# The scan's closing step of a quarter, with one multiply-and-add of 64 columns per head and term

## The reference

```python
y_diag = einsum('bcgij,bcgrij,bcjgr,bcjgrp->bcigrp', cb, decay, dt, x)
states = einsum('bcjgn,bcjgr,bcjgrp->bcgrpn', Bm, decay_to_end * dt, x)
h      = chunk_decay * h + states                  # carried from chunk to chunk
y_off  = einsum('bcign,bcigr,bcgrpn->bcigrp', Cm, exp(acs), h_prev)
y = y_f + flip(y_b) + d_skip[:, None] * xs         # forward, backward, skip
y = rms_norm(y * silu(z), ssd_norm)
```

## Time and profile before

| | |
|---|---|
| median of 3 runs | 1747.11 us (1747.05 to 1749.56) |
| the profiled execution | 1745.69 us, its span 1744.0 us |
| PE busy | 1610.1 us (92%) |
| VectorE busy | 1025.2 us (59%) |
| ScalarE busy | 675.2 us (39%) |
| GpSimd busy | 99.4 us (6%) |
| mean granted clock of PE | 0.96 of 2.4 GHz |
| chain that ended last | PE 76%, VectorE 12%, ScalarE 7% |

### The profile page before, as it was taken

One profiled execution on the slowest core, in us unless ns is written; L12 is line 12 of the kernel. 1 busy time (PEld: TensorE's weight loads), 2 busy tenths in 40 slices (PEclk: granted clock), 3 DMA queues, 4 the chain that ended last, 5 costly groups with the idle time before them and its releaser, 6 DMA issues.

```text
span 1744.0 us, 27356 instructions
## 1 busy us (share of the span) xinstructions
PE 1610.1 (92%) x11141; PEld 1525.7 (87%) x11141; DVE 1025.2 (59%) x1416; ACT 675.2 (39%) x1149; POOL 99.4 (6%) x155
## 2 busy tenths in 40 slices
PE   3699999998999899898979999999999999999998
PEld 2599999988999798888866579999989999999998
DVE  5476666664856467888856644334964253353468
ACT  4544444332446226666736543332432121121120
POOL 1000011110010110000000000000000000000000
PEclk9699999999999899999989999999999999999999
DMA  9244444443276766767661034534222222223231
GB/s 326 91 141 142 142 135 163 150 137 123 91 229 207 243 205 217 252 185 223 192 235 63 1 109 167 181 118 153 81 73 73 77 69 76 71 73 99 72 98 61
DMA packets 159747, 241.55 MB, mean 139 GB/s; under 512 B 8049, under 2 KB 126561, under 8 KB 156577
## 3 DMA queue, kind: packets, MB, share of 16 engines
q1 hardware_dynamic: 136464, 171.45, 30.3%
q0 software_dynamic: 12304, 47.72, 7.3%
q10 hardware_dynamic: 10880, 20.97, 4.5%
HBM read 195.06 MB, written 45.06 MB: 138 GB/s over the span
## 4 chain that ended last, share of the span: by engine, by line
PE 76%; DVE 12%; ACT 7%; issue 3%; DMA 1%; SPq 0%; ACTq 0%; DVEq 0%
PE acc L833 61%; PE tp L833 12%; DVE arena L2027 2%; ACT arena L1656 2%; ACT whi L1430 1%; PE tp L1215 1%; DVE wlo L1927 1%; DVE arena L2180 1%; DMA arena<-in_w_mod 1%; PE tp L916 1%; DVE wlo L1978 1%; DVE arena L2182 1%; DMA y_nat<-arena 1%; ACT arena L1442 1%; ACT whi L1793 1%
## 5 line engine op out<-in xcount | busy, mean ns | idle before, releaser
L833 PE MATMUL acc<-hh,whi 128*128 128x322 f32 x1152 | 305.2, 326 | 20.5 <-DVE wlo L1927 7.2
L833 PE MATMUL acc<-hl,whi 128*128 128x322 f32 x1152 | 299.1, 321 | 0.0
L833 PE MATMUL acc<-hh,wlo 128*128 128x322 f32 x1152 | 297.5, 320 | 0.0
L833 PEld LDWEIGHTS acc<-hh,whi 128*128 128x128 f32 x1152 | 210.0, 199 | 23.0 <-issue 10.4
L1927 DVE TENSOR_TENSOR wlo<-raw,whi 128x2048 fp32r<-128x2048 f32 x74 | 169.4, 2290 | 93.6 <-ACT whi L1430 93.6
L833 PEld LDWEIGHTS acc<-hl,whi 128*128 128x128 f32 x1152 | 210.4, 198 | 0.0
L833 PEld LDWEIGHTS acc<-hh,wlo 128*128 128x128 f32 x1152 | 209.9, 198 | 0.0
L1430 ACT ACTIVATE whi<-raw 128x2048 fp32r<-128x2048 f32 x74 | 141.0, 1907 | 167.0 <-PE acc L833 167.0
L833 PE MATMUL acc<-whi,hh 128*128 128x256 f32 x640 | 185.4, 290 | 0.0
L833 PE MATMUL acc<-wlo,hh 128*128 128x256 f32 x640 | 182.0, 284 | 0.0
L833 PE MATMUL acc<-whi,hl 128*128 128x256 f32 x640 | 182.0, 284 | 0.0
(11 more groups left out here) (292 smaller groups left out, 2948.9 us busy)
## 6 DMA issues: line engine op xcount, KB each, us to landing
raw<-in_w_in SPq DMA_DIRECT2D x38, 1024.0 KB, 7.0
raw<-in_w_mlp SPq DMA_DIRECT2D x32, 1024.0 KB, 5.2
arena<-in_w_mod SPq DMA_DIRECT2D x24, 1024.0 KB, 6.4
arena<-decay_sums_t ACTq DMA_DIRECT2D x40, 512.0 KB, 5.5
arena<-xs_nat SPq DMA_DIRECT2D x8, 1024.0 KB, 7.8
raw<-in_w_ssd_o SPq DMA_DIRECT2D x8, 1024.0 KB, 6.0
y_nat<-arena POOLq DMA_DIRECT2D x6, 1024.0 KB, 7.1
arena<-y_nat SPq DMA_DIRECT2D x6, 1024.0 KB, 6.0
```

The source lines that it names most:

```text
L833: return pe.matmul(out, l, r, start=first, stop=last)
```

## The change

`carried` is written with scalar_tensor_tensor, (a x s) + b, where s is one number per partition; so each instruction takes one head's 64 columns. The forward term stays one multiply over 512 columns. Then eight instructions (chunks 1 to 3 only) make hF = hF x decay + states, eight make y = backward x factor + y, and after a wait for them eight make y = x times skip + y. carried_ok is signalled by the last instruction of the backward term, and VectorE itself waits for it ahead of the skip term. The scratch tq and the helper `skipped` are still used by the context chunk.

```diff
@@ -2192,18 +2192,18 @@
                                     (("y_out0", 16), ("sq_ok", 8)))[c - 1]:
                         dve.wait_ge(s[name], n)
                 y = y_of(c)
-                dve.tensor_tensor(y[:, h], v(tp[:, 2]), f4(dec[:, c, 0], q), ALU.mult)
-                if c < NT - 1:
-                    do(dve.tensor_tensor(tq, v(tp[:, 3]), f4(dec[:, c, 0, NH:], q), ALU.mult))
-                    dve.tensor_tensor(hF[:, h], hF[:, h], f4(dec[:, c, 2], q), ALU.mult)
-                    do(dve.tensor_tensor(y[:, h], y[:, h], tq, ALU.add))
-                    dve.tensor_tensor(hF[:, h], hF[:, h], v(banks(q)[1]), ALU.add).then_inc(car["sem"], step(car))
-                else:
-                    dve.tensor_tensor(tq, v(tp[:, 3]), f4(dec[:, c, 0, NH:], q), ALU.mult).then_inc(car["sem"], step(car))
-                    dve.wait_ge(car["sem"], value(car))
-                    do(dve.tensor_tensor(y[:, h], y[:, h], tq, ALU.add))
-                skipped(b, q)
-                do(dve.tensor_tensor(y[:, h], y[:, h], tq, ALU.add))
+                forward, backward, states = v(tp[:, 2]), v(tp[:, 3]), v(banks(q)[1])
+                do(dve.tensor_tensor(y[:, h], forward, f4(dec[:, c, 0], q), ALU.mult))
+                for j, n in enumerate(range(8 * q, 8 * q + 8)):
+                    if c < NT - 1:
+                        dve.scalar_tensor_tensor(hF[:, n], hF[:, n], dec[:, c, 2, n:n + 1], states[:, j], ALU.mult, ALU.add)
+                for j, n in enumerate(range(8 * q, 8 * q + 8)):
+                    last = dve.scalar_tensor_tensor(y[:, n], backward[:, j], dec[:, c, 0, NH + n:NH + n + 1], y[:, n], ALU.mult, ALU.add)
+                last.then_inc(car["sem"], step(car))
+                dve.wait_ge(car["sem"], value(car))
+                for n in range(8 * q, 8 * q + 8):
+                    last = dve.scalar_tensor_tensor(y[:, n], xs[b][:, n], dsk[:, n:n + 1], y[:, n], ALU.mult, ALU.add)
+                do(last)
 
             def skipped(b, q):
                 do(dve.tensor_tensor(tq, xs[b][:, 8 * q:8 * q + 8], f4(dsk[:], q), ALU.mult))
```

## The result

| | before | changed |
|---|---|---|
| median | 1747.11 us (5 runs, 1744.25 to 1749.56) | 1754.85 us (5 runs, 1753.9 to 1758.79) |
| ratio | | 1.0048, 95% interval 1.0031 to 1.0064 |
| profiled execution, span | 1745.69, 1744.0 us | 1753.9, 1751.9 us |
| VectorE busy, instructions | 1025.2 us, 1416 | 1038.0 us, 1680 |
| PE busy | 1610.1 us | 1609.5 us |

The change makes the kernel slower by 0.48% by the ratio (8.4 us) and by 7.7 us by the medians; 1754.9 was forecast. VectorE is busy for 12.8 us more, and PE has the same work.

A forecast was written before the change was run, and what follows sets the result against it. No engine is full in the scan; PE and VectorE wait for each other, so added VectorE time counts only where PE waits. 6.6 us (chunks 1 to 3) plus 1.2 (chunk 4) on 1747.1 gave 1754.9 us, range 1749 to 1768.

The forecast's parts named there:

- The price of a short instruction: VectorE in `carried`: 64 columns with one scalar start 0.197 us apart; one lasts 0.279 us by itself.
- Rival two: Short VectorE instructions don't overlap: pitch 0.279 us, a quarter +2.8 us, total 1779 us, or 1787 with lowered clock; chance 0.08.
- rival four: Scalar's read hidden behind the instruction in front: pitch 0.134 us, a quarter 0.4 us shorter, total 1745 us; chance 0.08.
- The rule on PSUM: VectorE's cost per instruction: some 60 ns on SBUF, 125 ns on PSUM; the forecast took PSUM to cost nothing more.
- Rival three: PSUM adds 65 ns to each backward instruction: a quarter +1.5 us, 5.7 us more, total 1761 us; chance 0.06.
- The quarter: Eight heads' pass through `carried` in chunks 1 to 3: from 4.70 to 5.66 us, +0.96 us.
- The walk: Following VectorE's added time through chunk 3 to PE's waits: 2.2 us for each of three chunks, 1.2 us in chunk 4.
- the first quarter stays without effect: Chunk 3: its 0.96 us lands before VectorE's wait and beside PE's block; only the second quarter starts 0.6 us late.
- a second stretch at 0.50 in a chunk: Sign against the forecast: PE's granted clock at 0.50 (1.2 GHz) in a second place, instead of 1.00 behind the third quarter.
- rival 1: Scan lowers PE's clock at a second place, behind the third quarter: 2.5 us more, three times, total 1762 us; chance 0.19.
- the sum of 7.8: Latent scan's total growth: 6.6 us in chunks 1 to 3 plus 1.2 us in chunk 4.
- Nothing changed before 675 us and behind the scan: Sign for the forecast: the profile outside the latent scan stays as before, so the whole 7.8 us lies within it.

The follow-up runs named there:

- 32-column form: Changed kernel with the skip term cut into 16 instructions of 32 columns a quarter: 1769.28 against 1746.20 us for the kernel before, ratio 1.0132.
- two-quarter kernels: Kernel before with the new `carried` only in each chunk's first and second quarters (1748.03 us, ratio 1.0011), or only in the third and fourth (1754.45 us, 1.0046).
- kernel with the last two quarters: Kernel before with the new `carried` only in the third and fourth quarter of each chunk: 1754.45 us, ratio 1.0046.

## Why the prediction was right, and where it was not

- **The price of a short instruction** held. 0.197 us from start to start was worked out, and 0.192 (state, backward term) and (1.66 - 0.279) / 7 = 0.197 (skip term) measured; one lasts 0.268 to 0.286, 0.279 forecast. The 32-column form gives it once more: 2.69 us for 16 is some 0.16 apart, 0.033 for the columns and 0.13 besides. Rival two (no overlap) and rival four (the scalar's read hidden) are out. What the prediction quotes of the DRAIN from the Trainium skill, VectorE: DVE Perf Modes, is one half of what that section says: it goes on that a next instruction that isn't held starts earlier. The starts 0.192 us apart at a length of 0.274 agree with that half.
- **The rule on PSUM** that the prediction takes from the Trainium skill, Perfetto Trace Analysis, section Optimizing Scalar/DVE Operations, doesn't hold here: the eight backward instructions read PSUM in their first operand and take 1.62 us, the eight of the skip term read SBUF alone and take 1.66. Rival three is out.
- **The quarter**: 5.66 forecast, 5.60 measured.
- **The walk** held to some tenths. The waits of PE in front of group 4, of the bank release, of group 6 and of the products were forecast as 1.7, 1.0, 2.3 and 0.6, and were 2.15, 0.84, 2.15 and 0.66. Group 6 was forecast 1.6 late and was 1.33 late. That the first quarter stays without effect was not quite so: PE waited 0.40 for group 3. Chunk 1 was to take some 60 us and took 60.1. That it depends on where the time is added is shown: by the timed runs of the two-quarter kernels, whose intervals don't overlap, and by the full 1.04 us a quarter of the one with 32 columns. What the walk takes as fixed is not: the slack ahead of group 6 leaves 1.3 to 2.5 us a chunk of the change, as the clock behind group 1 had been in the kernel before, and the forecast of 1.6 lies in between.
- **The clock** is where the prediction failed in a part. It named "a second stretch at 0.50 in a chunk" as a sign that it was wrong, and all of chunks 1 to 3 had a second low stretch, in both profiles of the changed kernel: rival 1, at 19%. In chunk 1 it lay behind group 4, where VectorE was the limit, and cost nothing; in chunks 2 and 3 it lay behind group 6, and they took 61.6 and 61.7 us against chunk 1's 60.1. Chunk 3 grew by 3.8 us, where 2.2 was forecast: 1.33 up to group 6, 0.66 of wait for the products, 1.5 of clock behind group 6, and 0.25 from the products to the next group 1. Behind group 6 it costs 5.17 - 3.63 = 1.5 us each, where the rival had 2.5, because only part of the stretch is low. In chunk 4 it went the other way: group 6 and its filler took 6.3 us at the mixed clock and had taken 7.5 before (the chain: 1.97 + 5.53), so chunk 4 got 0.6 us shorter and not 1.2 longer. So the sum of 7.8 left out the clock, which took 1.5 us each in chunks 2 and 3 and gave some back in chunk 4. That the clock's falls follow from the longer waits is likely but not shown: the kernel before had one after a wait of 1.79 as well, and in the kernel with the last two quarters PE waited 2.15 us for group 6 in all of chunks 1 to 3, and the clock fell behind it in chunk 1 alone (6.1 us for the group and its filler, and 4.6 in the others).
- **"Nothing changed before 675 us and behind the scan"** was wrong as a statement on one execution. The scan of the changed kernel was 229.4 us long in both its profiles, that of before 219.9 and 218.7: 9.5 to 10.7 us more, not 7.8. In the first profiles the scan began 5.5 us earlier, and what lies behind it took 3.9 us longer (1751.9 - 899.23 against 1744.0 - 895.23), which comes to 7.9 in the spans. So the agreement to a tenth of a microsecond is luck: in the scan it rests on errors that went both ways, and outside it on shifts that the change didn't make. The timed runs bound the change at 5.4 to 11.2 us, with both 7.8 and 10 in it.

## What to carry to other kernels

Fusing two long passes into one multiply-and-add doesn't pay if it must be cut into a piece per head: count 0.13 us for each instruction with a per-partition scalar beside its columns, measured from start to start and not by the length of one. Then ask at which waits of the other engine the added time arrives: of the first 0.9 us in each of three quarters, 2.7 us, 1.3 to 2.5 arrived at group 6 here, and of the next 1.04 all 3.12, since the slacks were gone. A stretch of low clock on PE is to be read the same way: it costs nothing where PE waits for VectorE next, and 1.5 us where PE is the limit. The same view of waits shows what to do in place of it: moving one group of work ahead of a split that it doesn't need, and taking small stalls and the gate off the path, gave 14.8 us against the kernel before.

## What the runs showed of the hardware that was not expected

The kernel before took between 1739.4 and 1754.5 us in 24 runs on one chip, a spread of 0.9%. Two profiles of the same program put the start of the same group at 669.84 and 675.83 us, with a granted clock of 0.97 in both from 300 to 665 us, but 0.91 and 0.89 in the first 300. Effects of less than 5 us are better read from marks within the profile than from the total, and from several profiles: the same stretch from group 1 to group 6 took 28.4 to 29.6 us in six chunks, chunks 1 to 3 of two profiles, of one program.
